# Order of the matmuls in the MLP's panels: three tiles taken in turn in three PSUM banks at every block of weights

## The chip, the cores and the metric

The kernel runs on one core of one Trainium2 chip. The metric is the device time of one execution in microseconds, the median over several runs.

## The reference, cut to what matters

Two token streams (1024 prompt frames and 32 sample frames, 1056 in all) pass two layers. Layer 0 mixes with gMLP and RG-LRU heads, layer 1 with a short gated convolution. After each mixer comes the same MLP:

```python
hn = rmsnorm(x, p['norm_ffn_pre'][l])
f = jnp.square(jax.nn.relu(hn @ p['mlp_up'][l])) @ p['mlp_down'][l]
x = x + rmsnorm(f, p['norm_ffn_post'][l])
```

D_MODEL is 1024 and the hidden width 4096. Everything is float32.

## The kernel before, in words

The activations lie transposed in SBUF: a partition is a channel within a block of 128, the free axis holds the 1056 tokens, cut in NT = 3 tiles of TT = 352 tokens. A matrix product is made of **units**: a unit is one block of 128 output channels for one tile. Its contraction has KC = 8 blocks k, and each float32 product is made of three matmuls of 352 columns in the type fp32r: high weights with high activations (line 731), high weights with low activations (line 732), low weights with high activations (line 734). So a unit is 24 matmuls, which all accumulate in one PSUM bank; unit n takes bank n % 6 (`bank`, line 339; NB = 6). There are 552 units.

`plan()` (line 61) writes out the order of the units. `panel` makes three units in a row, tile 0, 1, 2, from one load of weights; `tile_block` makes four panels tile by tile, which means other weights at every unit. In an MLP (`mlp`, line 116) the first four panels are a tile block. Then follow four groups g of hidden channels: the up panels of the group (kind "up", 8 a group, 4 of them left in group 0), then 8 down panels (kind "dn0" in group 0, "dn" in groups 1 and 2) that contract over that group's hidden channels h. In group 3 an `out_group` (kind "dn3") takes their place: four panels and a tile block. Two MLPs start at units 72 and 360 (START[1] and START[3]). The first MLP's down groups begin at units 96, 144, 192 and 240, the second's at 384, 432, 480 and 528.

Each engine goes through the units in this order, written out by hand.

- TensorE (`unit`, line 704): waits for the low weights (`w_ready`), then for the evacuation of unit n - 6, which had the bank, then issues the 24 matmuls. The last one increments `pe_unit` (line 736). At the end of each block k, `between` (line 866) puts in small work at fixed places (the column sums and spreads of the norms, by the tables COL_AT and SPREAD_AT, and one transpose in unit START[3] + 30). For the down panels with m = 0, `h_part` (line 744) adds waits on `h_ready`, the count of finished low parts of h: at the first block of tile 0 for all tiles of every up panel but the last, at the last block (k = 7) for tile t of the last up panel.
- VectorE (loop at line 1731): at unit n it does `evacuate(n)` (line 1463), which waits for `pe_unit` n + 1 and, for "up", writes relu times the norm's factor to tmp (line 1473), for "dn0" copies to f (line 1476), for "dn" and "dn3" adds to f (line 1479). After that comes `h_low(n - 1)` (line 1748; function at line 1447, instruction at line 1450), the low part of h for the unit before, which increments `h_ready`. Then, where it is due, comes `low(l)` (line 1364, instruction at line 1367), the low part of a load of weights, which increments `w_ready`.
- ScalarE (loop at line 1300): at an up unit it squares tmp (line 1021) and casts it to h_hi (line 1023). Where it is due, `high(l)` (line 963, instruction at line 965) casts a load of weights once its DMA has landed.
- SyncE issues the weight loads (512 KB each). A load waits until the last unit that used its slot is done. Three slots rotate. `high(l)` stands six units ahead of the load's first unit, `low(l)` five units ahead.

The lines of the vector loop that matter:

```python
if kind not in SCALAR_OUT:
    evacuate(n)
...
if UNITS[n - 1].kind == "up" and n - 1 not in FIRST_TWO:
    h_low(n - 1)
```

Of the kernel before, what the change touches and what calls it, by code (L numbers as in the profile page):

```python
# [16 lines left out]
NT = 3  # L17
TT = TOK // NT
KC = D // P
# [9 lines left out]
NB = 6  # L29
# [130 lines left out]
def build(nc, A, O):  # L160
    UNITS, LOADS, START, OUT = plan()
    N_UNITS, N_LOADS = len(UNITS), len(LOADS)
# [16 lines left out]
    evac_no = []  # L179
# [8 lines left out]
    with ExitStack() as ctx:  # L188
        at_byte = [nc.sbuf_base + (-nc.sbuf_base) % 32]

        def place(name, shape, dt, offset=None):
            size = 4
            for n in shape[1:]:
                size *= n
            here = at_byte[0] if offset is None else offset
            if offset is None:
                at_byte[0] += size + (-size) % 32
            return nc.alloc_sbuf_tensor_at(name, shape, dt, offset=here)

        def sem(name):  # L200
            return ctx.enter_context(nc.semaphore(name))
# [3 lines left out]
        x_hi = place("x_hi", [P, CH], F32R)  # L205
        at_x_lo = at_byte[0]
        x_lo = place("x_lo", [P, CH], F32R)
        at_h_hi = at_byte[0]
        h_hi = place("h_hi", [P, CH], F32R)
        at_h_lo = at_byte[0]  # L210
        h_lo = place("h_lo", [P, CH], F32R)
# [77 lines left out]
        def pt(buf, c, t):  # L289
            return buf[:, c * TOK + t * TT:c * TOK + t * TT + TT]  # L290
# [34 lines left out]
        def w_k(l, which, k):  # L325
            v = W[l][which]
            if LOADS[l].slot in ("ha", "hb"):
                return v[:, k // 2, (k % 2) * P:(k % 2) * P + P]
            return v[:, k, :]
# [9 lines left out]
        def bank(n):  # L339
            return ps[:, n % NB, 0:TT]  # L340
# [3 lines left out]
        w_ready = sem("w_ready")  # L344
        pe_unit = sem("pe_unit")
        evac_d = sem("evac_d")
# [102 lines left out]
        COL_AT, SPREAD_AT = {}, {}  # L449
# [250 lines left out]
        def _(pe):  # L700
# [3 lines left out]
            def unit(n):  # L704
                u = UNITS[n]
                X = u.src == "X"
                src = (x_hi, x_lo) if X else (h_hi, h_lo)
                order = EVEN_ORDER if u.kind == "eo" else IN_ORDER
                l, t = u.load, u.t
                late = n < 4  # L710
                if n == 0:
                    pe.wait_ge(w_half, 1)
                elif late:
                    pe.wait_ge(w_high, l + 1)
                else:
                    pe.wait_ge(w_ready, l + 1)
                if n >= NB:
                    by_scalar = UNITS[n - NB].kind in SCALAR_OUT
                    pe.wait_ge(evac_a if by_scalar else evac_d, evac_no[n - NB] + 1)
                phase = START.index(max(s for s in START if s <= n))  # L720
                dst = bank(n)
                for i, k in enumerate(order):
                    if X and n - START[phase] in (0, 4, 8):
                        pe.wait_ge(x_ready, 24 * phase + 8 * t + k + 1)
                    if n == 0 and k == 4:
                        pe.wait_ge(w_high, 1)
                    if u.m == 0:
                        h_part(n, i)
                    hi, lo = pt(src[0], k, t), pt(src[1], k, t)
                    wh, wl = w_k(l, 0, k), w_k(l, 1, k)  # L730
                    nc.tensor.matmul(dst, wh, hi, start=(i == 0), stop=False)  # L731
                    nc.tensor.matmul(dst, wh, lo, start=False, stop=False)  # L732
                    if not late:
                        last = nc.tensor.matmul(dst, wl, hi, start=False, stop=(i == KC - 1))  # L734
                        if i == KC - 1:
                            last.then_inc(pe_unit, 1)
                    between(n, i)
                if late:
                    pe.wait_ge(w_ready, l + 1)
                    for k in range(KC):  # L740
                        last = nc.tensor.matmul(dst, w_k(l, 1, k), pt(src[0], k, t), start=False, stop=(k == KC - 1))  # L741
                    last.then_inc(pe_unit, 1)

            def h_part(n, i):

                kind, t = UNITS[n].kind, UNITS[n].t
                if kind in ("dn0", "dn", "dn3"):
                    done = index[n - 1 - t] + 1
                    if i == 0 and t == 0:
                        pe.wait_ge(h_ready, done - 3)  # L750
                    if i == KC - 1:
                        pe.wait_ge(h_ready, done - 2 + t)
                if kind == "oo":
                    if i == 0 and t == 0:
                        pe.wait_ge(y_ready, 21)
                    if i == KC - 1:
                        pe.wait_ge(y_ready, 22 + t)
                if kind == "eo":
                    if i == 0 and t == 0:
                        pe.wait_ge(mix_b, 12)  # L760
                    if i == 4 and t == 0:
                        pe.wait_ge(mix_a, 9)
                    if i == KC - 1:
                        pe.wait_ge(mix_a, 10 + t)
# [23 lines left out]
            def x_block(n, a):  # L788
                pe.wait_ge(x_in[n], 16)
                for k in range(KC):  # L790
                    last = nc.tensor.transpose(ps[:, a + k // 4, (k % 4) * P:(k % 4 + 1) * P],
                                               x_rows[:, n, k * P:(k + 1) * P], ident[:, :])
                last.then_inc(x0_t, 1)
# [144 lines left out]
            nc.tensor.transpose(ps[:, M1, 0:V_FIRST], vec_rows[0:V_FIRST, :], ident[0:V_FIRST, 0:V_FIRST]  # L938
                                ).then_inc(c_t, 1)
            x_block(2, 4)  # L940
            for n in range(N_UNITS):
                unit(n)

            B = BLOCK[3]
            pe.wait_ge(evac_d, evac_no[B + 7] + 1)
# [863 lines left out]
```

## Time and profile before

| | us |
|---|---|
| median of 3 runs | 2233.56 (2233.28 to 2234.76) |
| the profiled execution's own time | 2235.11 |
| its span, first to last instruction | 2233.3 |
| TensorE matmul busy | 2195.4 (98%) |
| TensorE weight load busy | 2178.9 (98%) |
| VectorE busy | 876.4 (39%) |
| ScalarE busy | 670.1 (30%) |
| GpSimd busy | 163.6 (7%) |

The profiled execution took 1.8 us more than its span and 1.55 us more than the median. Busy time of a pipelined engine counts any moment with an instruction under way, so 98% says that TensorE is hardly ever empty, not how densely its matmuls follow each other. That is read from the distance between their starts. A line of a timeline gives the start, the duration, the engine, the source line, the operation, what it writes and reads, shapes and count, and in brackets the idle time before it with what ended it.

### The profile page before, as it was taken

Reading aid. Unit: us, or ns where it says so; the run is one execution under the profiler, and the core shown is the slowest. Engines: PE = TensorE matmul, PEld = TensorE weight load, DVE = VectorE, ACT = ScalarE, POOL = GpSimd, SP = SyncE. Lnnn points to the kernel's source line nnn. Section 1 sums busy time; section 2 is a strip of 40 time slices with the busy share of each in tenths; the row PEclk is TensorE's granted clock in tenths of the full one; section 3 lists DMA queues with packets and bytes.
Section 4 is the critical chain, followed back from the end, with each engine's and each line's share of the span. In section 5 each row is a group of like instructions: output and inputs, shape, how many; then the busy total and the mean of one; then the engine's idle time right before and its main releaser. Section 6 shows DMA issues by size and latency. Waiting matters only on the chain.

```text
span 2233.3 us, 32210 instructions
## 1 busy us (share of the span) xinstructions
PE 2195.4 (98%) x13821; PEld 2178.9 (98%) x13821; DVE 876.4 (39%) x1349; ACT 670.1 (30%) x1143; POOL 163.6 (7%) x156
## 2 busy tenths in 40 slices
PE   8888999999999999999999999999999999999998
PEld 8888999999999999999999999999999999999997
DVE  5664328422322332333763333384223223323335
ACT  6454335411320320233521112354113103202333
POOL 1234200000000000000032323000000000000000
PEclk9999999999999999999999999999999999999999
DMA  6111313111111111114311113131111111111132
GB/s 214 42 34 30 123 51 116 48 41 46 48 48 48 48 48 48 40 46 135 99 55 48 48 48 134 39 116 48 48 49 43 43 48 48 48 48 48 52 121 78
DMA packets 228893, 143.02 MB, mean 64 GB/s; under 512 B 5248, under 2 KB 227408, under 8 KB 228752
## 3 DMA queue, kind: packets, MB, share of 16 engines
q1 hardware_dynamic: 228304, 140.89, 20.8%
q8 instruction: 110, 1.80, 0.3%
q14 instruction: 31, 0.25, 0.0%
q0 software_dynamic: 416, 0.07, 0.0%
q10 hardware_dynamic: 32, 0.01, 0.0%
HBM read 119.22 MB, written 21.73 MB: 63 GB/s over the span
## 4 chain that ended last, share of the span: by engine, by line
PE 95%; DVE 2%; ACT 2%; issue 1%; SPq 0%; DMA 0%; POOL 0%; DVEq 0%; POOLq 0%
PE ps L731 31%; PE ps L732 31%; PE ps L734 30%; PE ps L819 1%; PE ps L775 1%; DMA x_rows<-in_x_prompt_dram 0%; DVE xc L1560 0%; PE ps L847 0%; PE ps L784 0%; PE ps L860 0%; PE ps L741 0%; ACT L1187 0%; ACT lru L1187 0%; ACT lru L1189 0%; SPq L513 0%
## 5 line engine op out<-in xcount | busy, mean ns | idle before, releaser
L731 PE MATMUL ps<-x_hi,w_all 128*128 128x352 f32 x2328 | 763.8, 328 | 5.5 <-DVE w_all L1367 3.1
L732 PE MATMUL ps<-x_lo,w_all 128*128 128x352 f32 x2328 | 748.9, 322 | 0.0
L734 PE MATMUL ps<-x_hi,w_all 128*128 128x352 f32 x2304 | 741.1, 322 | 0.0
L731 PE MATMUL ps<-h_hi,w_all 128*128 128x352 f32 x1728 | 559.3, 324 | 0.8 <-DVE h_lo L1631 0.8
L734 PE MATMUL ps<-h_hi,w_all 128*128 128x352 f32 x1728 | 554.2, 321 | 0.0
L732 PE MATMUL ps<-h_lo,w_all 128*128 128x352 f32 x1728 | 554.1, 321 | 0.0
L731 PEld LDWEIGHTS ps<-x_hi,w_all 128*128 128x128 f32 x2328 | 438.6, 188 | 9.9 <-DVE w_all L1367 3.4
L732 PEld LDWEIGHTS ps<-x_lo,w_all 128*128 128x128 f32 x2328 | 439.9, 189 | 2.8 <-issue 1.0
L734 PEld LDWEIGHTS ps<-x_hi,w_all 128*128 128x128 f32 x2304 | 433.9, 188 | 0.0
L965 ACT CAST w_all<-w_all_raw 128x1024 fp32r<-128x1024 f32 x168 | 175.8, 1047 | 514.2 <-DMA w_all_raw<-in_mlp_down_dram 318.5
L731 PEld LDWEIGHTS ps<-h_hi,w_all 128*128 128x128 f32 x1728 | 324.2, 188 | 1.1 <-DVE h_lo L1631 1.0
L732 PEld LDWEIGHTS ps<-h_lo,w_all 128*128 128x128 f32 x1728 | 324.8, 188 | 0.0
L734 PEld LDWEIGHTS ps<-h_hi,w_all 128*128 128x128 f32 x1728 | 324.2, 188 | 0.0
L1473 DVE SCALAR_TENSOR_TENSOR tmp<-ps,rstd 128x352 f32<-128x352 f32 x192 | 100.4, 524 | 418.9 <-PE ps L734 418.9
L1021 ACT ACTIVATE tmp<-tmp 128x352 f32<-128x352 f32 x192 | 95.7, 498 | 465.6 <-DVE tmp L1473 465.2
L1479 DVE TENSOR_TENSOR f<-ps,f 128x352 f32<-128x352 f32 x144 | 75.5, 524 | 362.6 <-PE ps L734 362.5
L1367 DVE TENSOR_TENSOR w_all<-w_all_raw,w_all 128x1024 fp32r<-128x1024 f32 x169 | 208.0, 1231 | 20.5 <-ACT w_all L965 20.5
L1450 DVE TENSOR_TENSOR h_lo<-tmp,h_hi 128x352 fp32r<-128x352 f32 x192 | 99.2, 517 | 9.1 <-ACT h_hi L1023 9.1
L1023 ACT CAST h_hi<-tmp 128x352 fp32r<-128x352 f32 x192 | 93.5, 487 | 6.1
L1476 DVE COPY f<-ps 128x352 f32<-128x352 f32 x48 | 25.2, 525 | 138.2 <-PE ps L734 138.2
L1445 DVE TENSOR_TENSOR sq_sum<-sq_sum,tmp 128x352 f32<-128x352 f32 x84 | 43.8, 521 | 87.3 <-ACT tmp L1014 84.9
L731 PE MATMUL ps<-h_hi,x_hi 128*128 128x352 f32 x192 | 62.1, 323 | 0.0
(219 smaller groups left out, 1528.6 us busy)
## 6 DMA issues: line engine op xcount, KB each, us to landing
w_all_raw<-in_mlp_up_dram SPq DMA_DIRECT2D x60, 512.0 KB, 4.0
w_all_raw<-in_mlp_down_dram SPq DMA_DIRECT2D x60, 512.0 KB, 4.1
x_save<-f SPq DMA_DIRECT2D x12, 1408.0 KB, 6.3
x_old<-x_save SPq DMA_DIRECT2D x12, 1408.0 KB, 11.4
w_all_raw<-in_c_w_in_dram SPq DMA_DIRECT2D x22, 512.0 KB, 3.8
w_all_raw<-in_w_in_even_dram SPq DMA_DIRECT2D x15, 512.0 KB, 3.9
x_rows<-in_x_prompt_dram SPq DMA_DIRECT2D x8, 512.0 KB, 6.7
w_all_raw<-in_w_out_even_dram SPq DMA_DIRECT2D x6, 512.0 KB, 4.3
```

Of the source, the lines that this page charges most:

```text
L731: nc.tensor.matmul(dst, wh, hi, start=(i == 0), stop=False)
L732: nc.tensor.matmul(dst, wh, lo, start=False, stop=False)
L734: last = nc.tensor.matmul(dst, wl, hi, start=False, stop=(i == KC - 1))
L965: nc.scalar.copy(W[l][0], W[l][2]).then_inc(w_high, 1)
L1021: nc.scalar.activation(tmp[n % 3][:, :], tmp[n % 3][:, :], ACT.Square).then_inc(h_sq, 1)
L1023: nc.scalar.copy(pt(h_hi, u.m, u.t), tmp[n % 3][:, :]).then_inc(h_high, 1)
L1367: nc.vector.tensor_tensor(lo, raw, hi.bitcast(F32), ALU.subtract).then_inc(w_ready, 1)
L1445: nc.vector.tensor_tensor(dst, dst, tmp[n % 3][:, :], ALU.add).then_inc(f_acc, 1)
L1450: nc.vector.tensor_tensor(pt(h_lo, u.m, u.t), tmp[n % 3][:, :], pt(h_hi, u.m, u.t).bitcast(F32), ALU.subtract).then_inc(h_ready, 1)
L1473: ins = nc.vector.scalar_tensor_tensor(tmp[n % 3][:, :], bank(n), 0.0, scale, ALU.max, ALU.mult)
L1476: ins = nc.vector.tensor_copy(pt(f, m, t), bank(n))
L1479: ins = nc.vector.tensor_tensor(pt(f, m, t), bank(n), pt(f, m, t), ALU.add)
```

## The change

`panel(n)` issues three units of one load together. For each block k and for each of the three products it goes through the three tiles, each in its own bank; so the 9 matmuls of a block k are high-high for tiles 0, 1, 2, high-low for tiles 0, 1, 2, low-high for tiles 0, 1, 2. Each tile's last matmul increments `pe_unit`, in the last three matmuls of the panel. The panel waits once for its weights and once for the evacuation of unit n - 4, the last that used its three banks. It is taken for kinds "up", "dn0" and "dn" where three units share a load, except for down panels with m = 0 and for panels that hold one of the places of small work. Everything else stays with `unit`. No other engine's program is changed.

```diff
--- before.py
+++ after.py
@@ -741,6 +741,21 @@
                         last = nc.tensor.matmul(dst, w_k(l, 1, k), pt(src[0], k, t), start=False, stop=(k == KC - 1))
                     last.then_inc(pe_unit, 1)
 
+            def panel(n):
+
+                u = UNITS[n]
+                src = (x_hi, x_lo) if u.src == "X" else (h_hi, h_lo)
+                pe.wait_ge(w_ready, u.load + 1)
+                pe.wait_ge(evac_d, evac_no[n + 2 - NB] + 1)
+                for k in range(KC):
+                    wh, wl = w_k(u.load, 0, k), w_k(u.load, 1, k)
+                    for p, (w, part_no) in enumerate(((wh, 0), (wh, 1), (wl, 0))):
+                        for t in range(NT):
+                            last = nc.tensor.matmul(bank(n + t), w, pt(src[part_no], k, t), start=(k == 0 and p == 0),
+                                                    stop=(k == KC - 1 and p == 2))
+                            if k == KC - 1 and p == 2:
+                                last.then_inc(pe_unit, 1)
+
             def h_part(n, i):
 
                 kind, t = UNITS[n].kind, UNITS[n].t
@@ -938,8 +953,17 @@
             nc.tensor.transpose(ps[:, M1, 0:V_FIRST], vec_rows[0:V_FIRST, :], ident[0:V_FIRST, 0:V_FIRST]
                                 ).then_inc(c_t, 1)
             x_block(2, 4)
-            for n in range(N_UNITS):
-                unit(n)
+            busy = {n for n, i in list(COL_AT) + list(SPREAD_AT)} | {START[3] + 30}
+            n = 0
+            while n < N_UNITS:
+                three = UNITS[n:n + 3]
+                if (three[0].kind in ("up", "dn0", "dn") and len({u.load for u in three}) == 1
+                        and not (three[0].kind != "up" and three[0].m == 0) and not busy & {n, n + 1, n + 2}):
+                    panel(n)
+                    n += 3
+                else:
+                    unit(n)
+                    n += 1
 
             B = BLOCK[3]
             pe.wait_ge(evac_d, evac_no[B + 7] + 1)
```

## Rows read from the trace of the kernel before

**Rows 1.** The page: busy time by engine, and the chain that ended last.

```profile
PE 2195.4 (98%) x13821; PEld 2178.9 (98%) x13821; DVE 876.4 (39%) x1349; ACT 670.1 (30%) x1143; POOL 163.6 (7%) x156
...
PE 95%; DVE 2%; ACT 2%; issue 1%; SPq 0%; DMA 0%; POOL 0%; DVEq 0%; POOLq 0%
```

**Rows 2.** Windows of the MLPs: us, busy (x instructions), PEclk, DMA share, GB/s.

```profile
408.80:958.50 549.70, 549.70 (x3459) 549.70 (x3458) 162.85 (x267) 120.94 (x196) 0.00 (x0) 1.00 0.16 47
1522.00:2072.00 550.00, 550.00 (x3460) 549.95 (x3460) 162.93 (x267) 121.26 (x197) 0.00 (x0) 1.00 0.16 47
```

**Rows 3.** Timeline of PE: the starts of units 96 and 99, one panel apart.

```profile
454.81 0.32 PE L731 MATMUL ps<-h_hi,w_all 128*128 128x352 f32 x1
...
466.26 0.32 PE L731 MATMUL ps<-h_hi,w_all 128*128 128x352 f32 x1
```

**Rows 4.** Timeline of PE: end of unit 93, start of unit 94.

```profile
446.86 0.32 PE L732 MATMUL ps<-x_lo,w_all 128*128 128x352 f32 x1
447.02 0.32 PE L734 MATMUL ps<-x_hi,w_all 128*128 128x352 f32 x1
447.18 0.32 PE L731 MATMUL ps<-x_hi,w_all 128*128 128x352 f32 x1
```

**Rows 5.** Timeline of DVE: units 93 and 94.

```profile
447.38 0.53 DVE L1473 SCALAR_TENSOR_TENSOR tmp<-ps,rstd 128x352 f32<-128x352 f32 x1 [2.86 <-PE ps L734]
447.82 0.52 DVE L1450 TENSOR_TENSOR h_lo<-tmp,h_hi 128x352 fp32r<-128x352 f32 x1
451.20 0.53 DVE L1473 SCALAR_TENSOR_TENSOR tmp<-ps,rstd 128x352 f32<-128x352 f32 x1 [2.86 <-PE ps L734]
451.64 0.52 DVE L1450 TENSOR_TENSOR h_lo<-tmp,h_hi 128x352 fp32r<-128x352 f32 x1
452.07 1.22 DVE L1367 TENSOR_TENSOR w_all<-w_all_raw,w_all 128x1024 fp32r<-128x1024 f32 x1
```

**Rows 6.** Timeline of ACT: unit 93.

```profile
447.94 0.50 ACT L1021 ACTIVATE tmp<-tmp 128x352 f32<-128x352 f32 x1 [2.80 <-DVE tmp L1473]
448.47 0.49 ACT L1023 CAST h_hi<-tmp 128x352 fp32r<-128x352 f32 x1
448.86 1.05 ACT L965 CAST w_all<-w_all_raw 128x1024 fp32r<-128x1024 f32 x1
```

**Rows 7.** The page, DMA issues: out<-in, queue, count, KB, us to landing.

```profile
w_all_raw<-in_mlp_up_dram SPq DMA_DIRECT2D x60, 512.0 KB, 4.0
```

**Rows 8.** Timeline of DVE ahead of a wait of PE, in unit 48.

```profile
263.93 2.13 DVE L1631 TENSOR_TENSOR h_lo<-mixed,h_hi 128x352 fp32r<-128x352 f32 x3
```

**Rows 9.** Timeline of PE at that wait.

```profile
265.04 0.32 PE L734 MATMUL ps<-h_hi,w_all 128*128 128x352 f32 x1
266.12 0.43 PE L731 MATMUL ps<-h_hi,w_all 128*128 128x352 f32 x1 [0.76 <-DVE h_lo L1631]
266.39 0.32 PE L732 MATMUL ps<-h_lo,w_all 128*128 128x352 f32 x1
266.55 0.32 PE L734 MATMUL ps<-h_hi,w_all 128*128 128x352 f32 x1
```

**Rows 10.** Timeline of PE: the starts of units 83, 84, 85 and 86.

```profile
404.99 0.32 PE L731 MATMUL ps<-x_hi,w_all 128*128 128x352 f32 x1
...
408.86 0.32 PE L731 MATMUL ps<-x_hi,w_all 128*128 128x352 f32 x1
...
412.73 0.33 PE L731 MATMUL ps<-x_hi,w_all 128*128 128x352 f32 x1
...
416.60 0.32 PE L731 MATMUL ps<-x_hi,w_all 128*128 128x352 f32 x1
```

**Rows 11.** The page: the matmuls of the three products with h.

```profile
L731 PE MATMUL ps<-h_hi,w_all 128*128 128x352 f32 x1728 | 559.3, 324 | 0.8 <-DVE h_lo L1631 0.8
L734 PE MATMUL ps<-h_hi,w_all 128*128 128x352 f32 x1728 | 554.2, 321 | 0.0
L732 PE MATMUL ps<-h_lo,w_all 128*128 128x352 f32 x1728 | 554.1, 321 | 0.0
```

**Rows 12.** Windows, columns as rows 2, of a stretch at the lower clock.

```profile
76.70:78.60 1.90, 1.90 (x8) 1.90 (x7) 0.00 (x0) 0.13 (x1) 0.00 (x0) 0.50 0.00 0
```

**Rows 13.** Timeline of PE in that stretch.

```profile
76.91 0.50 PE L731 MATMUL ps<-x_hi,w_all 128*128 128x352 f32 x1
77.20 0.50 PE L732 MATMUL ps<-x_lo,w_all 128*128 128x352 f32 x1
```

## The prediction

> **What bounds the kernel now.** I read the page first. TensorE has a matmul under way 98% of the time and the chain that ended last is PE for 95% [rows 1]. VectorE is busy 39%, ScalarE 30%, so faster evacuation as such is worth nothing. What counts is how densely the matmuls follow each other, and where TensorE waits. In the two MLP stretches of 550 us, 3459 and 3460 matmuls start [rows 2]: 549.70 / 3459 = 158.9 ns each, no idle time, granted clock 1.00, the upper of the two levels (2.4 GHz). One panel, from the start of unit 96 to the start of unit 99, is 466.26 - 454.81 = 11.45 us [rows 3] for 72 matmuls, 159.0 ns each. The 352 columns alone would be 352 / 2.4 = 146.7 ns at that clock, so some 12 ns of each interval are something else: weight loads (one to each matmul, 13821 of both [rows 1]) or the hand-over. Of the whole, the change concerns 97 panels: 28 up panels and 24 down panels a MLP, less 3 down panels with m = 0, twice, less the one that holds the transpose of unit 390. None of the norms' places of small work lies in a panel (the last is in unit 81 and 369, the first panels begin at 84 and 372). 97 x 72 = 6984 matmuls, 1110 us, half of the span.
>
> **The change, part by part.** Nothing is removed and nothing added on TensorE but waits: the same matmuls and as many weight loads, in another order. Three things move.
>
> **1. The matmuls' interval, taken as unchanged: 0 us.** The trace has no row with a new tile and a new bank at every matmul. It has one at every unit's end: the last matmul of unit 93 starts at 447.02, the first of unit 94, in another bank and tile, at 447.18, and the one before the last at 446.86 [rows 4]. All 0.16: changing the bank and the tile costs nothing and frees nothing that shows. So I take 159.0 ns for the new order too. This is the term that I know least, and 1 ns is worth 6984 x 1 = 7.0 us. The same matmuls are not always equally fast, though nothing is waited for: unit 83 takes 408.86 - 404.99 = 3.87 us and units 84 and 85 3.87 us each [rows 10], 161.2 ns a matmul against 159.0 [rows 3]. So there is a rhythm between matmuls and weight loads with at least two levels. The upper one would cost 6984 x 2.2 = 15 us. Below, the bound is the columns alone, 6984 x (159.0 - 146.7) = 86 us less; the nearest rows lie far from that end, as the interval at the change of bank is no shorter, so I take nothing of it.
>
> **2. The three evacuations come at once, at the panel's end: 0 us for banks and weights.** The last matmul of each tile starts two, one and no interval before the panel's last. VectorE then needs, per tile, an evacuation of 0.53 and an h_low of 0.52, spaced 0.44 us [rows 5], and once a panel the low part of a load, 1.22. ScalarE has a square and a cast a tile, 0.50 + 0.49, and once the high part, 1.05 [rows 6]. Call T the panel's end, when the next panel would start. The evacuation of tile 0 starts about T - 0.12 (below), the square 0.56 later (447.94 - 447.38), the cast 0.53 after that, the high part at T + 1.4, to T + 2.4. The low part is behind it, to T + 3.7, and the third evacuation and its h_low behind that, about T + 4.7. The banks and those weights are needed by the panel after the next, at T + 11.45: 6.8 us of cover. In down panels there is less to do. The weights' DMA is issued when its slot is free, one panel before T, and takes 4.0 us [rows 7] of 11.45. If this cover were gone, each panel would wait for what is left of the chain. Gaps that panels could fill are not there either, since the stretches of [rows 2] have none.
>
> **3. A new wait at each group of down panels: 8 x 1.17 = +9.3 us.** The down panel with m = 0 stays with the old routine, and its first matmul waits until h_low is done for every up panel but the last, the last tile of the last panel but one included (unit 92 for unit 96). VectorE issues that h_low(92) behind evacuate(93) (its order is evacuate(n), then h_low(n - 1)), and evacuate(93) waits for unit 93. Before, unit 93 ended two units ahead of unit 96, 7.6 us, and nobody noticed. As a panel, unit 93 ends only with units 94 and 95, so h_low(92), ready for a whole panel, sits behind a wait for the panel's end. Step by step. The evacuation starts 447.38 - 447.18 = 0.20 us after the next matmul's start [rows 4, 5]; unit 93's last matmul is now two intervals earlier, so it starts at T + 0.20 - 2 x 0.16 = T - 0.12. h_low(92) follows 0.44 later and takes 0.52 [rows 5]: done at T + 0.84. From the end of VectorE's work to TensorE's first matmul, the one wait of the same kind in the trace shows 266.12 - (263.93 + 2.13) = 0.06 us [rows 8, 9], and that first matmul holds the next up by 0.27 instead of 0.16, another 0.11. Together 0.84 + 0.06 + 0.11 = 1.01 us. Behind a disturbance the units run at the slower rhythm until the tile has changed a few times ([rows 10] stand behind the norms' small work): 3 units x 24 x 2.2 ns = 0.16. So 1.17 us, at units 96, 144, 192, 240 and 384, 432, 480, 528. Queued behind the waiting matmul is all of TensorE. The next condition, h_low(93) at block k = 7, is due 21 matmuls, 3.4 us, into unit 96, at T + 4.3, and is done by about T + 2: covered. Bounds: 0 if the wait falls away after all, and 8 x (1.17 + 1.14) = 18 us if a low part of weights (1.22 us, [rows 5]) came in front; that is placed at unit 94, behind, so I take 1.17.
>
> **The sum.** Profiled execution 2235.1 + 0 + 0 + 9.3 = 2244.4 us; the profile stood 1.55 us over the median of the runs, 2233.56, so in terms of the median 2242.9, say 2243. About 0.2%, 4.5 us, is what a measurement of this kernel can tell from no change.
>
> **The rivals.**
>
> Slower rhythm. The new order locks at the slower level of [rows 10] through the panels: +15 us, 2258. For it: each change of tile seems to move the rhythm (unit 85, the first after units of tile 0 alone, is no faster), and the new order changes it at every matmul. Against it: twelve units on, with tiles changing at every unit, the level is 159.0 again [rows 3]. Chance 0.23.
>
> Faster rhythm, the other side. If matmuls to alternating banks let the next one start sooner, the interval falls below 159.0. From 9.3 / 6984 = 1.3 ns less it outweighs the waits; from 2.0 ns less (157.0) the kernel is faster by more than 0.2%. At 156 ns: 2243 - 21 = 2222. For it: 12 ns over the columns' 146.7 are unexplained and could be accumulation in one bank. Against it: the first matmul in a new bank is no sooner [rows 4]. Chance 0.14.
>
> The waits don't come. If h_low(92) were done in time, or if a bit of pace pays for them, nothing measurable is left: 2234. Against it: the order written in VectorE's program. Chance 0.10.
>
> Repeated weights. Six matmuls in a row now use the same weights. If a second load of what is there cost less, the interval could fall towards 146.7: 2243 - 86 = 2157. Against it: line 732 already repeats the weights of line 731, has its own load (as many loads as matmuls [rows 1]), and takes 321 ns as line 734 with new weights does [rows 11]. Chance 0.03. The Trainium skill ("TensorE: Matmul & The Clock Gate", Part 2, the step on LDWEIGHTS) says that weights can stay put over many matmuls, loaded once. By that the change could gain; the rows show a load to every matmul, so here it does not.
>
> The clock falls. A change of bank at every matmul could open small gaps in which the granted clock drops to 1.2 GHz. At clock 0.50 [rows 12] matmuls start 77.20 - 76.91 = 0.29 us apart [rows 13], 0.13 more than now; a quarter of the panels' matmuls in that state is 1746 x 0.13 = 230 us, 2473. Against it: every unit changes the bank and the clock stays at 1.00 [rows 2]. Chance 0.03. The Trainium skill has this rule in the same page, "A second HAM failure mode: psum-queue depth-cycling": cycling through PSUM banks each iteration left TensorE short idle times, and its clock swung between the levels. It speaks against this change.
>
> **How the numbers follow.** My forecast, waits of about 1.2 us and an unchanged interval, has 0.45; the cases above have 0.23, 0.14, 0.10, 0.03, 0.03, and 0.02 are left for something else. Its own range is 2238 to 2248 (0.7 ns of interval either way). The range over all reaches down to 2228, which takes in the case without waits and the milder half of the faster rhythm, and up to 2260 for the slower rhythm: about 0.15 stay out. Slower: 0.45 + 0.23 + 0.03, less a little, 0.70. Same: 0.10 and edges, 0.14. Faster: 0.16.
>
> **What would show it.** Eight waits of TensorE for h_lo, line 1450, of about 0.9 us each, at the first matmul of units 96, 144 and so on, and no other new ones; 11.45 us from panel to panel; clock 1.00; VectorE's three evacuations in a bunch. I am wrong if the panels take other than 11.4 to 11.5 us, or if the waits are absent or number in the tens.

## The result and the profile after

The changed kernel takes 2267.9 us (median of 4 runs, 2266.34 to 2268.05) against 2233.56: a ratio of 1.0151, 95% interval 1.0134 to 1.0169. It is 34.3 us slower. I had forecast slower, at 2243, with a range up to 2260; the direction was right and the size was not.

The profiled execution took 2267.84 us, its span is 2266.0 us. The page's busy times and chain, to be held against [rows 1]:

```profile
PE 2219.3 (98%) x13821; PEld 2200.4 (97%) x13821; DVE 868.5 (38%) x1349; ACT 663.9 (29%) x1143; POOL 163.4 (7%) x156
...
PE 95%; DVE 2%; ACT 2%; issue 1%; POOL 0%; DMA 0%; DVEq 0%; POOLq 0%; ACTq 0%
...
L754 PE MATMUL ps<-x_hi,w_all 128*128 128x352 f32 x2688 | 510.5, 324 | 3.7 <-DVE w_all L1391 3.7
...
L731 PE MATMUL ps<-h_hi,w_all 128*128 128x352 f32 x744 | 242.5, 326 | 7.3 <-DVE h_lo L1474 6.5
```

As many matmuls and weight loads as before. TensorE is busy 24 us longer and idle 9 us longer. The lines have moved: 754 is the panel's matmul, 1474 is h_low (1450 before), 1391 is low (1367), 1497 the evacuation (1473). TensorE's waits in the changed kernel (who for whom: us in total, times, longest):

```profile
PE ps L731 <- DVE h_lo L1474: 6.5, 8, 0.8
...
PE ps L754 <- DVE w_all L1391: 3.7, 2, 1.9
PE ps L731 <- DVE w_all L1391: 3.1, 1, 3.1
```

The last row was there before. The eight waits for h_lo are those of the forecast. The two for weights are not. Now the interval, by which I mean the mean distance between the starts of two matmuls that follow each other; single distances scatter by some ns around it. Units 147 to 167 are seven panels, 504 matmuls, in which nothing waits. Their first start and the next panel's first, before and after (timeline of PE):

```profile
649.40 0.32 PE L731 MATMUL ps<-h_hi,w_all 128*128 128x352 f32 x1
...
729.53 0.32 PE L731 MATMUL ps<-x_hi,w_all 128*128 128x352 f32 x1
```

```profile
657.66 0.32 PE L754 MATMUL ps<-h_hi,w_all 128*128 128x352 f32 x1
...
739.24 0.32 PE L754 MATMUL ps<-x_hi,w_all 128*128 128x352 f32 x1
```

(729.53 - 649.40) / 504 = 158.99 ns a matmul before, (739.24 - 657.66) / 504 = 161.87 after; from the starts in nanoseconds it is 158.98 and 161.85. The mean over all 97 panels before was 159.03.

All 97 panels together took 1110.7 us before and 1143.9 after, 33.2 more; the rest of the kernel took 0.5 less. The 33.2 come apart like this, each term the excess of the panels concerned, worked out from the starts in the trace:

| | us |
|---|---|
| interval: 6984 matmuls x (161.85 - 159.03) ns | 19.7 |
| eight waits for h_lo behind the last up panel of a group: 8 x 0.985 | 7.9 |
| two waits for weights at units 87 and 375: 2 x 2.01 | 4.0 |
| a stretch at the lower clock behind the first of these | 1.6 |

The waits in close-up. VectorE at the end of the panel 93 to 95, and TensorE's first matmuls of unit 96 (timelines of the changed kernel):

```profile
457.69 0.53 DVE L1497 SCALAR_TENSOR_TENSOR tmp<-ps,rstd 128x352 f32<-128x352 f32 x1 [7.00 <-PE ps L754]
458.13 0.52 DVE L1474 TENSOR_TENSOR h_lo<-tmp,h_hi 128x352 fp32r<-128x352 f32 x1
458.56 0.52 DVE L1497 SCALAR_TENSOR_TENSOR tmp<-ps,rstd 128x352 f32<-128x352 f32 x1
```

```profile
458.79 0.40 PE L731 MATMUL ps<-h_hi,w_all 128*128 128x352 f32 x1 [0.82 <-DVE h_lo L1474]
459.03 0.32 PE L732 MATMUL ps<-h_lo,w_all 128*128 128x352 f32 x1
```

VectorE is idle for 7.00 us while h_low(92) could be done, since it stands waiting in evacuate(93). h_low(92) ends at 458.65, TensorE's matmul starts at 458.79. At unit 87 the same, with weights in h_low's place:

```profile
419.09 0.52 DVE L1497 SCALAR_TENSOR_TENSOR tmp<-ps,rstd 128x352 f32<-128x352 f32 x1 [9.87 <-PE ps L754]
419.53 0.52 DVE L1474 TENSOR_TENSOR h_lo<-tmp,h_hi 128x352 fp32r<-128x352 f32 x1
419.96 1.22 DVE L1391 TENSOR_TENSOR w_all<-w_all_raw,w_all 128x1024 fp32r<-128x1024 f32 x1
```

```profile
421.23 0.75 PE L754 MATMUL ps<-x_hi,w_all 128*128 128x352 f32 x3 [1.86 <-DVE w_all L1391]
```

The second panel of each MLP uses weights whose low part is due at the first panel's first unit, 84 (372 in the second MLP), and stands behind that unit's evacuation, so behind the panel's end, just when the next panel wants them. Behind the wait of 1.86 us the granted clock fell in the first MLP and not in the second, where the wait was as long (windows: us, busy by engine, clock, DMA share, GB/s):

```profile
422.20:425.30 3.10, 3.10 (x13) 3.10 (x12) 1.85 (x3) 1.44 (x3) 0.00 (x0) 0.50 0.18 55
1552.70:1556.00 3.30, 3.30 (x22) 3.30 (x21) 2.52 (x5) 2.05 (x5) 0.00 (x0) 1.00 0.41 122
```

### The profile page after: what moved, and what is told of

The parts are those of the page before. It is cut to its first block, busy times and chain, and to the rows that moved or that the text cites. A ratio compares the mean times of both kernels' runs of the same rounds, so it can differ in the third digit from the quotient of the medians.

```text
span 2266.0 us, 32016 instructions
## 1 busy us (share of the span) xinstructions
PE 2219.3 (98%) x13821; PEld 2200.4 (97%) x13821; DVE 868.5 (38%) x1349; ACT 663.9 (29%) x1143; POOL 163.4 (7%) x156
## 4 chain that ended last, share of the span: by engine, by line
PE 95%; DVE 2%; ACT 2%; issue 1%; POOL 0%; DMA 0%; DVEq 0%; POOLq 0%; ACTq 0%
PE ps L754 50%; PE ps L731 14%; PE ps L732 14%; PE ps L734 14%; PE ps L834 1%; PE ps L790 1%; PE ps L806 0%; DVE xc L1584 0%; PE ps L862 0%; PE ps L799 0%; PE ps L875 0%; DVE h_lo L1474 0%; PE ps L741 0%; ACT L1211 0%; ACT lru L1213 0%
## 5 line engine op out<-in xcount | busy, mean ns | idle before, releaser
L754 PE MATMUL ps<-x_hi,w_all 128*128 128x352 f32 x2688 | 510.5, 324 | 3.7 <-DVE w_all L1391 3.7
L754 PEld LDWEIGHTS ps<-x_hi,w_all 128*128 128x128 f32 x2688 | 448.7, 189 | 4.3 <-DVE w_all L1391 4.3
L754 PE MATMUL ps<-h_hi,w_all 128*128 128x352 f32 x1968 | 372.9, 323 | 0.0
L731 PE MATMUL ps<-x_hi,w_all 128*128 128x352 f32 x984 | 329.8, 335 | 5.5 <-DVE w_all L1391 3.1
L754 PEld LDWEIGHTS ps<-h_hi,w_all 128*128 128x128 f32 x1968 | 327.9, 188 | 0.0
L732 PE MATMUL ps<-x_lo,w_all 128*128 128x352 f32 x984 | 317.8, 323 | 0.0
L734 PE MATMUL ps<-x_hi,w_all 128*128 128x352 f32 x960 | 309.5, 322 | 0.0
L754 PE MATMUL ps<-x_lo,w_all 128*128 128x352 f32 x1344 | 290.1, 324 | 0.0
L731 PE MATMUL ps<-h_hi,w_all 128*128 128x352 f32 x744 | 242.5, 326 | 7.3 <-DVE h_lo L1474 6.5
L734 PE MATMUL ps<-h_hi,w_all 128*128 128x352 f32 x744 | 239.3, 322 | 0.0
L732 PE MATMUL ps<-h_lo,w_all 128*128 128x352 f32 x744 | 238.7, 321 | 0.0
L754 PEld LDWEIGHTS ps<-x_lo,w_all 128*128 128x128 f32 x1344 | 228.8, 188 | 0.0
L754 PE MATMUL ps<-h_lo,w_all 128*128 128x352 f32 x984 | 211.9, 323 | 0.0
L731 PEld LDWEIGHTS ps<-x_hi,w_all 128*128 128x128 f32 x984 | 186.4, 189 | 9.4 <-issue 3.7
L732 PEld LDWEIGHTS ps<-x_lo,w_all 128*128 128x128 f32 x984 | 187.3, 190 | 2.8 <-issue 1.0
L734 PEld LDWEIGHTS ps<-x_hi,w_all 128*128 128x128 f32 x960 | 181.1, 189 | 0.0
L754 PEld LDWEIGHTS ps<-h_lo,w_all 128*128 128x128 f32 x984 | 167.0, 188 | 0.0
```

Source lines behind the costliest of these rows:

```text
L754: last = nc.tensor.matmul(bank(n + t), w, pt(src[part_no], k, t), start=(k == 0 and p == 0), stop=(k == KC - 1 and p == 2))
```

## The experiments

**Are the waits and the interval two separate costs?** VectorE's order is mended (`first_of_panel` holds the first unit of each panel; the later places of `h_low` and `low` are left out for these units):

```diff
+                if n in first_of_panel:
+                    if UNITS[n - 1].kind == "up":
+                        h_low(n - 1)
+                    for l in range(4, N_LOADS):
+                        if low_at[l - 4] == n and l not in EARLY_LOW:
+                            low(l)
...
                     evacuate(n)
```

> The changed kernel with VectorE's order mended: where unit n begins a panel, h_low(n - 1) and the low parts of weights that are due at n stand ahead of evacuate(n). Theory: the new waits and the longer interval are two separate costs. Then the eight waits for h_lo (1.06 us each, 8.5 us) and the two waits for weights at units 87 and 375 (2.1 us each, with 1.6 us of lower clock behind the first) go away, 14.4 us in all: 2253.5 us, and the panels stay at 161.85 ns a matmul. Rival A: the waits only cover something else that is late, so the time stays above 2262. Rival B: the longer interval is an effect of the waits' disturbance; then the panels go back to 159.0 ns too and the time is about 2234.

2254.44 us (2252.01 to 2256.26, 4 runs) against 2234.28: ratio 1.0093, 95% interval 1.0077 to 1.0110. The ten waits are gone, the clock stays at 1.00 from 408 to 960 us, the panels keep 161.85 ns:

```profile
650.32 0.32 PE L754 MATMUL ps<-h_hi,w_all 128*128 128x352 f32 x1
...
731.89 0.32 PE L754 MATMUL ps<-x_hi,w_all 128*128 128x352 f32 x1
```

The panels take 1130.3 us, 13.6 less than in the changed kernel; 14.4 were expected. Two separate costs: 13.5 of the 34.3 us are VectorE's order, the rest, 20 us, is the interval.

**Bank, tile, or the repeated weights?** Three kernels pull the new order apart. They compute something else in the panels, as their expectations say, and each ran once, with its profile. VectorE's order is the changed kernel's.

```diff
-    last = nc.tensor.matmul(bank(n + t), w, pt(src[part_no], k, t), ...
+    last = nc.tensor.matmul(bank(n + t), w, pt(src[part_no], k, 0), ...   e2_bank_only
+    last = nc.tensor.matmul(bank(n), w, pt(src[part_no], k, t), ...       e3_tile_only
+    last = nc.tensor.matmul(bank(n), w, pt(src[part_no], k, 0), ...       e4_repeat_only
```

> The changed kernel, but all three banks of a panel get tile 0's activations (it computes tile 0 three times in the panels and leaves tiles 1 and 2 out). Banks still turn at every matmul, the moving operand's tile doesn't. Bank theory: the panels stay at 161.85 ns a matmul. Tile theory (the address of the moving operand): they go to 159.0 ns or at least below 160. Weights theory (the same weights six times, then three times, instead of two and one): 161.85 ns.

> The changed kernel, but all 72 matmuls of a panel go to the first unit's bank, which sums the three tiles; the other two banks are not written, and pe_unit is raised by three at the end. Tiles still turn at every matmul, the bank doesn't. Bank theory: the panels go to 159.0 ns a matmul. Tile theory: they stay at 161.85 ns. Weights theory: 161.85 ns.

> The changed kernel with one bank and tile 0 alone in a panel: each matmul is issued three times over, with the change's order of weights (six uses of the high ones, three of the low ones). Bank theory and tile theory: 159.0 ns a matmul. Weights theory: 161.85 ns. If this is slow and e2 and e3 are too, it is the order of the weights and products.

The starts of units 147 and 168, e2, then e3, then e4:

```profile
655.05 0.32 PE L754 MATMUL ps<-h_hi,w_all 128*128 128x352 f32 x1
...
735.41 0.32 PE L754 MATMUL ps<-x_hi,w_all 128*128 128x352 f32 x1
```

```profile
659.21 0.32 PE L754 MATMUL ps<-h_hi,w_all 128*128 128x352 f32 x1
...
740.78 0.32 PE L754 MATMUL ps<-x_hi,w_all 128*128 128x352 f32 x1
```

```profile
655.65 0.32 PE L754 MATMUL ps<-h_hi,w_all 128*128 128x352 f32 x1
...
736.01 0.32 PE L754 MATMUL ps<-x_hi,w_all 128*128 128x352 f32 x1
```

159.44 ns with the banks turning and the tile fixed, 161.85 with the tiles turning and the bank fixed, 159.44 with neither. In each pair the bank turns once and once it doesn't, and the interval is the same to the hundredth of a nanosecond. The bank theory is out. The tile, which is to say the address that the moving operand (the activations, here) is read from, makes 2.41 of the 2.87 ns. For the remaining 0.46 ns (159.44 against 158.98) there are two candidates: the order of weights and products, and the order of addresses, since a block k now lasts nine matmuls in place of three.

**What of the address?** Two tiles are 1408 bytes apart, blocks k 4224 bytes. Both are odd multiples of 128. So tile t of block k starts on a multiple of 256 bytes when t + k is even and 128 bytes off one when it is odd. The high and low buffers of x and h lie 33792 bytes apart, a multiple of 256. Where I wrote "a multiple of 256 bytes", it is counted from the buffer's start; I did not determine where that itself stands.

```diff
-    pt(src[part_no], k, t)
+    pt(src[part_no], k, (0, 2, 0)[t])    e5_tiles_020
+    pt(src[part_no], k, (0, 1, 0)[t])    e6_tiles_010
```

> The changed kernel, but the three matmuls of a product take the activations of tiles 0, 2, 0 instead of 0, 1, 2 (tile 1 is left out of the panels, tile 0 computed twice); the banks turn. Tiles start 1408 bytes apart, five and a half times 256, so tile 1 starts half way between two multiples of 256 bytes where tiles 0 and 2 start on one, and the other way round at every second block k. Alignment theory: with tiles 0 and 2 the moving operand keeps its alignment within a block k, and the interval is that of tile 0 alone, 159.44 ns (e2, e4). Any-change theory (each jump of the address costs): 161.85 ns.

> As before, but tiles 0, 1, 0: the alignment turns at each matmul as in the change. Alignment theory: 161.8 ns, give or take 0.3, since the alignments follow each other exactly as in tiles 0, 1, 2. Any-change theory: 161.85 ns as well. If it stands near 159.4, both are wrong and something of the distance of 2816 bytes counts.

The same two starts, e5, then e6:

```profile
655.11 0.32 PE L754 MATMUL ps<-h_hi,w_all 128*128 128x352 f32 x1
...
735.47 0.32 PE L754 MATMUL ps<-x_hi,w_all 128*128 128x352 f32 x1
```

```profile
659.56 0.32 PE L754 MATMUL ps<-h_hi,w_all 128*128 128x352 f32 x1
...
741.13 0.32 PE L754 MATMUL ps<-x_hi,w_all 128*128 128x352 f32 x1
```

159.44 and 161.85 ns. Jumps of 2816 bytes between tiles 0 and 2 cost nothing, with jumps of 1408 the interval is 2.4 ns longer. The any-change theory is out, and the alignment modulo 256 fits every kernel with panels so far. One word of the expectations is wrong: neither in e6 nor in the change does the alignment turn at each matmul. Each product ends on the alignment that the next one begins with, so there are two turns in a product and one on to the next block: it turns at seven matmuls of nine, in both kernels alike.

**Turning, or the level of each alignment?**

```diff
-    pt(src[part_no], k, t)
+    pt(src[part_no], k - k % 2, 0)    e9_all_on
+    pt(src[part_no], k - k % 2, 1)    e10_all_off
```

> The changed kernel, but every matmul of a panel takes activations that start on a multiple of 256 bytes: tile 0, and the even block below k in place of an odd one (tiles 1 and 2 and the odd blocks are left out of the panels). Turning theory: what costs is that the alignment changes from one matmul to the next, so with no change at all this and the next run both stand under the 159.44 ns of e2, at the same value. Level theory: one of the two alignments is slow in itself; then this run and the next differ, one below and one above 159.44 ns.

> The same with tile 1 for tile 0: every matmul of a panel takes activations that start 128 bytes off a multiple of 256. Turning theory: the same value as e9, under 159.44 ns. Level theory: another value than e9.

The same two starts, e9, then e10:

```profile
655.55 0.32 PE L754 MATMUL ps<-h_hi,w_all 128*128 128x352 f32 x1
...
736.75 0.32 PE L754 MATMUL ps<-x_hi,w_all 128*128 128x352 f32 x1
```

```profile
654.58 0.32 PE L754 MATMUL ps<-h_hi,w_all 128*128 128x352 f32 x1
...
734.38 0.32 PE L754 MATMUL ps<-x_hi,w_all 128*128 128x352 f32 x1
```

And e9 at units 99 and 120, seven panels apart as well:

```profile
470.10 0.32 PE L754 MATMUL ps<-h_hi,w_all 128*128 128x352 f32 x1
...
550.74 0.32 PE L754 MATMUL ps<-x_hi,w_all 128*128 128x352 f32 x1
```

e10 runs at 158.33 ns in every panel without a wait or a lower clock. e9 runs at 161.11 ns in units 147 to 167 and at 160.00 in units 99 to 119 and most others, nowhere under 159.9. So the turning theory's equal values did not come, and e9 is not under 159.44 as it said. Each alignment has a level of its own, and one of them is slower by 1.7 to 2.8 ns. But 161.85, with both alignments in equal parts, is over both levels, and 2.1 to 2.7 ns over their mean (159.2 to 159.7): the order of the alignments costs on top. The level theory got the pair right and does not explain 161.85; the turning theory has it the other way round. Nor is it the number of turns as such. In the kernel before the alignment turns at every third matmul, and that runs at 158.98.

The pair also bears on the 0.46 ns. e10 uses each weight block as often in a row as e2 and e4 do, and it is faster than the kernel before (158.33 against 158.98). e2, e4 and e5, at 159.44, lie within the mean of the two levels. So repeated weights need not cost anything.

**Orders that turn less, with nothing left out and VectorE's order as in e1.**

```diff
+                        for t in (0, 2, 1):                      e8_order_021, the tiles in a product
...
-                    for p, (w, part_no) in enumerate(...):
-                        for t in range(NT):
+                    for t in range(NT):                          e7_tile_by_tile
+                        for p, (w, part_no) in enumerate(...):
```

> Correct kernel: VectorE's order as in e1, the panel as in the change but with the tiles in the order 0, 2, 1 (0, 1, 2 in the last product alone, since the counts go by it). Alignment theory: the alignment turns once or twice in three matmuls instead of two or three times, the interval falls below 161.85, to between 159.5 and 161. Any-change theory: 161.85 ns.

One run, 2254.44 us, as much as e1's median. Units 147 to 167 take 161.39 ns a matmul: less than 161.85, but above the 161 that I had allowed. The alignment turns at 42 matmuls of a panel's 72 in place of 56, and that helped by half a nanosecond at most.

> Correct kernel: VectorE's order as in e1, and in each block k the panel does the three products of tile 0, then of tile 1, then of tile 2, so the tile and the bank turn at every third matmul and the weights are used as before the change (high, high, low). Each turn costs by itself: a third of the 2.41 ns stays and the 0.46 ns of the repeated weights go, 159.8 ns, about 2240 us. Rival (a rhythm with few levels, in which the panels lock): one of the levels seen, 158.98 or 161.1 ns, so 2234 or 2249 us.

2235.65 us (10 runs, 2235.17 to 2239.89) against 2235.05: ratio 1.0006, 95% interval 0.9996 to 1.0016, no difference from the kernel before. Here the rival was right. The panels lock in one of a few rhythms: 161.11 ns in the first four panels of each MLP, 160.00 in the 15 that follow in the first MLP and the one that follows in the second, and 158.89 in the other 73. The kernel before passes nearly the same values behind the norms' small work: unit 83 has 161.08, unit 87 160.00, unit 88 158.88. Units 147 and 168:

```profile
649.72 0.32 PE L754 MATMUL ps<-h_hi,w_all 128*128 128x352 f32 x1
...
729.80 0.32 PE L754 MATMUL ps<-x_hi,w_all 128*128 128x352 f32 x1
```

The bank turns every third matmul and the tile too, and the interval is 0.1 ns below that of the kernel before. The alignment turns at every third matmul, as it did before the change. So neither three open banks nor three evacuations at once cost anything that shows.

The last kernel of this kind sorts the 24 pairs of block and tile:

```diff
+                for k in range(0, KC, 2):
+                    off, on = [(k + 1, 0), (k, 1), (k + 1, 2)], [(k, 0), (k + 1, 1), (k, 2)]
+                    pairs += on + off if k % 4 == 2 else off + on
```

> Correct kernel: VectorE's order as in e1, the three products of one tile and block together as in e7, and the 24 pairs of block and tile sorted so that the alignment of the activations stays the same for 9 or 18 matmuls at a time. If an alignment has its own pace (e9: 160.0 to 161.1 ns, e10: 158.33 ns) and a turn costs something on top, the panels run at the mean of the two, 159.2 to 159.7 ns, or a little under, since the repeated weights of e9 and e10 are gone: 2235 to 2240 us. If only turns cost, less than e7's 158.89 ns and under 2234 us.

2237.39 us (10 runs) against 2234.62: ratio 1.0010, 95% interval 1.0001 to 1.0020. Units 147 and 168:

```profile
648.91 0.32 PE L758 MATMUL ps<-h_hi,w_all 128*128 128x352 f32 x1
...
729.29 0.32 PE L758 MATMUL ps<-x_hi,w_all 128*128 128x352 f32 x1
```

That is 159.48 ns, and all panels but two stand at 159.3 to 159.7, as if each alignment ran at its own level. The order high, high, low of the weights is that of the kernel before, and the interval is still 0.5 ns longer. So holding one alignment for nine matmuls or more goes with the longer interval without any repeated weights. No gain over e7 or over the kernel before, and none of the versions that compute the right thing beats it.

**The waits with the old interval.** e7's order of matmuls, VectorE's order left as the change leaves it.

> Correct kernel: the changed kernel with the three products done tile by tile in a block k, as in e7, but with VectorE's order left as it was. The two costs are additive: e7's 2235.7 us and the 13.5 us by which e1 lies under the changed kernel, 2249 us, with eight waits for h_lo of 0.8 us and two for weights of 1.9 us, and panels at 158.9 to 161.1 ns as in e7. Rival: the disturbance by the waits throws the rhythm to a slower level for good; then over 2255 us.

2239.94 us (8 runs) against 2234.13: ratio 1.0028, 95% interval 1.0017 to 1.0038. That is 4 us over e7, not 13.5. The waits are there, but shorter:

```profile
PE ps L754 <- DVE w_all L1391: 2.4, 2, 1.2
PE ps L731 <- DVE h_lo L1474: 1.5, 8, 0.2
```

My expectation overlooked when tile 0 ends. In the changed kernel its last matmul stands two places before the panel's last, here six, 0.64 us earlier, and VectorE's chain starts that much sooner. 0.82 - 0.64 = 0.18 is the 0.2 us of the row. The waits for weights shrink alike, from 1.9 to 1.2. That confirms the mechanism better than equal waits would have: the wait is the chain of evacuate(n) and h_low(n - 1), less the lead of tile 0.

The 4 us understate the waits. By the starts in the trace they lengthen e11's panels by 5.8 us (11.9 in the changed kernel). But behind its first wait, at unit 87 and again at 375, e11 keeps 158.89 ns, the later waits aside, also in the 22 panels there that run at 161.11 or 160.00 in e7, which gives back 2.2 us. Units 99 and 120 of e11, where e7 runs at 160.00:

```profile
466.96 0.32 PE L754 MATMUL ps<-h_hi,w_all 128*128 128x352 f32 x1
...
547.04 0.32 PE L754 MATMUL ps<-x_hi,w_all 128*128 128x352 f32 x1
```

So the rival, a disturbance that makes the rhythm slower for good, is out: behind the waits the panels hold the fastest rhythm of this order.

## Why the prediction was right in direction and wrong in size

**The waits at the down groups** came as worked out: eight, at units 96, 144, 192, 240 and 288 units on. The panel's end is lengthened by 0.985 us, and the start of the second matmul behind it by another 0.08, 1.06 together; 1.01 was forecast. h_low(92) ends 0.84 us behind the panel's end, as worked out; from there to the matmul it is 0.14 us instead of 0.06. With slower units behind the wait I had 1.17. That slower rhythm did not come: units 96 to 98 run at 160.3 ns on average instead of 159.0, which is 0.1 us, and 0.08 of it are the held-up start. So 8.5 us instead of 9.3. e1 removes the waits and shows that VectorE's order alone makes them. They are a quarter of the 34.3 us; the direction was right for this reason, but most of the loss came from elsewhere.

**The cover for banks and weights** was the second step, taken at 0. It holds in 95 panels. It failed at units 87 and 375. I had let a load's low part stand five units ahead of its first use. For the load of the second panel of each MLP it stands three units ahead, because its slot is freed late, by a unit of the tile block (`high_at` is the larger of free + 1 and first - 6). I had read the rule for the steady case and not its first members. It cost 4.0 us, and 1.6 us for the lower clock.

**The interval** is the step that failed: term 1, taken as unchanged at 0 us, cost 19.7 us. I argued that changing the bank and the tile at a unit's end costs nothing. For the bank that was right, and e2 to e4 show it. For the tile, one change in 24 matmuls told nothing: an effect that depends on the order of alignments over several matmuls does not show in one distance rounded to 0.01 us, while 2.8 ns on each of 6984 matmuls is 20 us. The row that I leaned on [rows 4] could not show it in any case: unit 93 ends with tile 0 and block 7, unit 94 begins with tile 1 and block 0, both 128 bytes off a multiple of 256. Tile and bank change there, the alignment does not. The rival of the slower rhythm, at 0.23, had the right kind of cost. Its reading of [rows 10] was loose, since unit 85 follows units of tiles 2 and 0, not of tile 0 alone. It was priced at 2258, from the 161.2 ns of [rows 10]; the panels settled at 161.85, which no steady stretch of the kernel before shows. With the rival's interval priced right and my own waits the sum would have been 2233.6 + 19.7 + 8.5 = 2261.8, and with the two waits for weights and the clock 2267.4, against 2267.9 measured. The upper end of the range, 2260, held the slower rhythm with the eight waits, but no second surprise beside it, and the waits for weights had no case of their own.

**The faster rhythm** did not come, and its reason, accumulation in one bank, is refuted: turning the bank gives 159.44 and 159.44. **The repeated weights** gain nothing: there is still a load to every matmul, and with tile 0 alone (e4) the interval is 159.44 ns. Whether they cost anything is open. **The waits stay away** was wrong. **The clock** fell once inside the panels, behind the wait at unit 87, and not through the banks. The changed kernel turns the bank at every matmul through this stretch and keeps 1.00:

```profile
660.00:820.00 160.00, 160.00 (x991) 160.00 (x989) 41.28 (x69) 30.18 (x49) 0.00 (x0) 1.00 0.16 45
```

The Trainium skill ("TensorE: Matmul & The Clock Gate", "A second HAM failure mode: psum-queue depth-cycling") tells of a kernel that cycled through its banks, had short idle times between its groups of matmuls, and whose clock swung. The trace here shows no such swings: the banks turn, but TensorE is busy for 160.00 of the 160.00 us, and the clock stays.

What stays open: why an address off by 128 bytes in 256 changes the distance of matmuls at all, why one alignment is slower, why turns that stand one or two matmuls apart cost more than turns three apart, and how the steady rhythms of e7 and e9 come about. The runs show the dependence, not the mechanism inside the chip. The 0.46 ns were not isolated by a run of their own; e10 and e12 point to the order of the alignments and away from the repeated weights.

## What to carry to other kernels

When units that ended one by one are made to end together, look in the other engines' programs for work that is queued behind a wait for the first of them. What was ready earlier now waits for the group's end, and whoever needs it waits too. Moving it ahead of the wait, as e1 does, took the ten waits away and brought no new ones. Look at the first members of a schedule by themselves, since their lead can be shorter than the steady one. When a kernel is bound by its matmuls and has thousands of them, a change of their order is a change of their pace until shown otherwise: multiply a nanosecond by their number before calling it nothing. Ask also whether the row that shows "no cost" holds the thing that the change does: here it had a new tile and a new bank, but no new alignment. In this kernel the alignment of the moving operand was part of the order, through tile and block strides that are odd multiples of 128 bytes.

## What the runs showed of the hardware that I had not expected

- Matmuls of 352 columns in fp32r, with a weight load each and nothing waited for, run at mean distances between 158.33 and 161.85 ns, by the order in which their moving operands are addressed. Over units 147 to 167 the values repeat to 0.01 ns across kernels with the same order of alignments (e2, e4 and e5: 159.44; the changed kernel, e1, e3 and e6: 161.85).
- The distance depends on the moving operand's start modulo 256 bytes, at the two places 128 bytes apart that the runs try: 158.33 ns at one alignment always (e10), 160.00 or 161.11 at the other (e9), 161.85 when it turns at seven matmuls of nine. When it turns at every third it is 158.98 (before) and 158.89 to 161.11 (e7).
- The same order can hold different steady rhythms in different stretches (e7: 161.11, 160.00, 158.89), and stays in one over many panels. Which one can depend on what came before: e11, the same order with waits, holds 158.89 behind its first wait.
- Changing the PSUM bank at every matmul costs nothing and gains nothing (159.44 ns with and without, 161.85 with and without).
- Of two equal waits of TensorE of 1.86 us one was followed by a stretch at the lower level (0.50 in 422.20 to 425.30 us), one by none (1.00 in 1552.70 to 1556.00).
